# Six context value groups move from the placing stage into the latent routing

## The chip, the cores and the metric

The kernel runs on one core of a Trainium2 chip. The metric is the device time of one launch in microseconds (us). The core has a matmul engine (PE, its weight loads listed as PEld), a vector engine (DVE), an activation engine (ACT), a general-purpose engine that issues the indirect gathers (POOL), and a sequencer for plain transfers (SP). ACT can issue plain transfers too.

## The reference, cut to what matters

The layer ends, for each of 1280 tokens (1024 latent ones, 256 context ones), in a sum over product-key experts:

```
s = einsum('nhpd,pkd->nhpk', q, sub_keys)
s_top, i_top = top_k(s, 16)
...
best, best_pos = top_k(cand, 16)
expert = idx1 * 128 + idx2            # 8 heads x 16 = 128 experts a token
act = gelu(einsum('cd,ced->ce', x_c, u[e_c]))
out = einsum('ce,ced->cd', g_c * act, v[e_c])
```

So a token needs 128 rows of `u` (one dot product each) and 128 rows of `v` (a weighted sum), each of 1024 float32 numbers. A gather of one row for 128 partitions moves 512 KB.

## The kernel before, in words

Tokens are split into ten tiles of 128. Four latent tiles are computed densely, against all experts; four latent and two context tiles (`CONTEXT_GATHER = 2`) gather the rows of the experts they picked. This text is about the second half of that work, the **value sum**, for the two context tiles.

A value group is four tokens. For each of its tokens POOL issues one indirect gather of the 128 rows of `v` that the token picked (one row on each partition), and PE adds them up in eight matmuls (four tokens by two halves of 512 columns), with weights that hold the token's factors in one column. A context tile has 32 groups, so the two have 64. They are computed in two places:

- **In the latent routing** (`routing` with the group LAT, line 1579 on). The class `Values` (line 441) lists the units (tile, group) and cuts the last `LATE_GROUPS` of them off the list (line 452): 64 - 14 = 50 are left. Gathers are in `gather_values` (line 488, the DMA on line 495), products in `value_products` (line 501, matmuls on line 509). The rows lie in a ring of three groups (`VALUE_GROUPS = 3`): the gather of group m waits until the products of group m - 3 are done. POOL has nothing else to do in this stage. PE's products are woven into its other work by hand: 38 of them between the query products (`VALUES_IN_PART`, line 1597), two before each of four transposes of tokens, one after, and **all that are left** at the very end, after the transposes of the expert ids (line 1752). Then ACT takes the sums out of PSUM (`values_out`, line 516, the copy on line 521), SP stores them, and the stage ends with a barrier for all engines. DVE's work in this stage is the top-k search for the latent tokens; its last instruction is the copy of the shares on line 1996.
- **In the placing stage** (`place_weights`, line 2000). This stage turns the routing of the four dense tiles into a dense grid of weights in HBM, in 4 tiles x 8 = 32 steps. In each step DVE makes one-hot rows (lines 2136 to 2151), ACT scales some (2241 to 2255), PE multiplies them (2196), ACT copies the result into the grid (2263). After every eight steps SP stores a tile of the grid, 8 MB (line 2288), the last tile in two halves. Beside that, POOL gathers 24 rows of `u` (line 423) and DVE makes a dot product of each (line 432). The late groups ride along: in every odd step POOL issues four late gathers (line 2092, ring of six rows), and PE makes the products of one group between batches 1 and 2 of the step (`late_products`, line 2171, matmuls on line 2177).

When the last late group is done, at step `LATE_STEPS = 2 * LATE_GROUPS = 28`, ACT asks for the 2 MB load `h2T` into the room in which late rows had landed (2225), copies the sums out of PSUM (2227) and issues four stores of them (2231). Two steps later it waits for these stores and asks for the first two slabs of `u` of the expert stage (2235). Each step's body on ACT runs in the order: scale batch 0, copy batches 2 and 3 of the step before, `late_values` (line 2220), batch 2, copy batches 0 and 1.

The lines that set the sizes and the late part:

```
VALUE_GROUPS = 3                                             # line 437
LATE_GROUPS = 14                                             # line 438
        del self.units[-LATE_GROUPS:]                        # line 452, Values
            values(len(values_left))                         # line 1752, PE, end of routing
        GROUPS = range(P // 4 - LATE_GROUPS, P // 4)         # line 2027, place_weights
        LATE_STEPS = 2 * LATE_GROUPS                         # line 2028
                    if b == 2 and before % 2 and before < LATE_STEPS:
                        late_products(before // 2)
```

Of the kernel before, what the change touches and what calls it, by code (L numbers as in the profile page):

```python
# [434 lines left out]


VALUE_GROUPS = 3
LATE_GROUPS = 14


class Values:
# [4 lines left out]
    def __init__(self, scope, signals, out, last_row):  # L446
# [4 lines left out]
        self.units = [(k, q) for k in range(CONTEXT_GATHER) for q in range(self.GROUPS)]  # L451
        del self.units[-LATE_GROUPS:]
        self.per_tile = [len([u for u in self.units if u[0] == k]) for k in range(CONTEXT_GATHER)]
# [1546 lines left out]
def place_weights(nc, io, keep, scratch, routes, ahead, edge):  # L2000
# [13 lines left out]
    with Scope(nc, "place") as s:  # L2014
# [11 lines left out]
        out = edge.late_row[0]  # L2026
        GROUPS = range(P // 4 - LATE_GROUPS, P // 4)
        LATE_STEPS = 2 * LATE_GROUPS
        ps = [s.psum(f"ps{n}", [P, SLAB]) for n in range(BATCHES)]
# [54 lines left out]
        def _(pool):  # L2084
            def gather_late(rows):
                for i in rows:
                    if i >= 4 * LATE_GROUPS:
                        return
# [73 lines left out]
        def _(pe):  # L2162
# [8 lines left out]
            def late_products(g):  # L2171
# [3 lines left out]
                for t in range(4):  # L2175
                    for half in range(2):
                        last = nc.tensor.matmul(
                            v_ps[QUAD * t:QUAD * (t + 1), half * SLAB:(half + 1) * SLAB], factor_col[:, g % 2, t, :],
                            late_row[(4 * g + t) % LATE_RING][:, half * SLAB:(half + 1) * SLAB],
                            start=(g == 0), stop=(g == LATE_GROUPS - 1), tile_position=(0, QUAD * t))  # L2180
                last.then_inc(values_done, 1)
# [20 lines left out]
        def _(act):  # L2202
            def factor_column(g):
                if g >= 2:
                    act.wait_ge(values_done, g - 1)
                    nc.scalar.activation(factor_col[:, g % 2, :, GROUPS[g - 2]], factorT[:, 0:4], ACT.Copy, scale=0.0)
                q = GROUPS[g]
                nc.scalar.activation(factor_col[:, g % 2, :, q], factorT[:, 4 * q:4 * q + 4], ACT.Copy)\
                  .then_inc(column_ready, 1)
# [10 lines left out]
            def late_values(before):  # L2220
                if before % 2 == 0 and before // 2 + 1 < LATE_GROUPS:
                    factor_column(before // 2 + 1)
                if before == LATE_STEPS:
                    act.wait_ge(values_done, LATE_GROUPS)
                    nc.scalar.dma_start(keep["acc"][:, :, :].rearrange("p t n -> p (t n)").rearrange("p (k n) -> p k n", k=KD),
                                        scratch["h2T"]).then_inc(edge.h2_in, 16)
                    nc.scalar.activation(out, v_ps[:, :], ACT.Copy).then_inc(late_ready, 1)
                    act.wait_ge(late_ready, 1)
                    for t in range(4):
                        rows = slice(QUAD * t + GROUPS[0], QUAD * (t + 1))  # L2230
                        nc.scalar.dma_start(scratch["ffn"][CTX.first + 1][rows, :], out[rows, :]).then_inc(late_stored, 16)
                if before == LATE_STEPS + 2:
                    act.wait_ge(late_stored, 64)
                    for n in range(2):
                        nc.scalar.dma_start(edge.u_raw[:, n, :, :], io["uT"][n]).then_inc(edge.u_in[n], 16)
# [885 lines left out]
```

## Time and profile before

| what | value |
|---|---|
| median of 3 runs | 3383.41 us (3379.23 to 3384.15) |
| the profiled execution's own time | 3384.96 us |
| its span in the profile | 3383.1 us |
| latent routing, value sums of the context | about 1000 to 1386 us of the span |
| placing | 1386 to 1608 us |
| experts | 1609 us to the end |

The profile is of one execution; its time and its span differ by 1.9 us, which lies around the first and the last instruction. All places in time below are microseconds from the start of the span. A line such as `1372.50 0.94 POOL L495 ... [0.30 <-issue]` reads: start, duration, engine, line of the kernel, and in brackets how long the engine had been idle before it and what ended that.

### The profile page before, as it was taken

What the parts mean: (1) busy time and instruction counts of PE and PEld (TensorE: products, weight loads), DVE (VectorE), ACT (ScalarE), POOL (GpSimd) and SP (SyncE); (2) the same over time, 40 slices, a digit from 0 to 9 for tenths busy, and PEclk for the clock granted to TensorE, in tenths of its full rate; (3) what the DMA queues carried; (4) which work ended last, traced back from release to release, by engine and by line L of the source; (5) the groups of instructions that cost most, each with busy time, mean ns of one, the idle gap of its engine ahead of it and who ended that gap; (6) DMA issues with size and microseconds to landing.
All of it is one profiled execution on the core that took longest, in us unless ns stands there. A gap on an engine that the chain in (4) does not pass through costs nothing.

```text
span 3383.1 us, 46093 instructions
## 1 busy us (share of the span) xinstructions
PE 3094.1 (91%) x15031; PEld 2033.5 (60%) x15031; DVE 2658.1 (79%) x5943; ACT 1058.5 (31%) x1909; POOL 1984.7 (59%) x1674
## 2 busy tenths in 40 slices
PE   6989899799899998677699999999999999999996
PEld 4747345666454444455455677776677767677674
DVE  2328899787587999798698878887788888787788
ACT  4741344465121111577211222222222222222222
POOL 0000577444454566543588777787777777777771
PEclk8989999999999999899899999999999999999998
DMA  9441788765967888799999999999999999999997
GB/s 337 174 147 61 250 305 298 208 204 162 356 242 268 298 290 320 289 360 360 355 387 384 411 413 413 413 413 411 413 413 413 413 412 413 413 414 413 410 412 309
DMA packets 365084, 1131.17 MB, mean 334 GB/s; under 512 B 31945, under 2 KB 98761, under 8 KB 356609
## 3 DMA queue, kind: packets, MB, share of 16 engines
q0 software_dynamic: 221184, 805.40, 62.4%
q1 hardware_dynamic: 135248, 316.40, 24.6%
q10 hardware_dynamic: 8496, 7.44, 0.7%
q8 instruction: 80, 1.31, 0.2%
q14 instruction: 76, 0.61, 0.1%
HBM read 1075.93 MB, written 53.19 MB: 334 GB/s over the span
## 4 chain that ended last, share of the span: by engine, by line
PE 25%; DMA 11%; POOL 6%; issue 5%; DVE 4%; ACT 0%; POOLq 0%; SPq 0%; DVEq 0%; ACTq 0%
PE exp_a_ps L2601 12%; DMA exp_value_row<-in_v_rows,exp_v_id 9%; PE exp_o_ps L2628 8%; PE exp_v_ps L2585 4%; POOL exp_value_row L2757 3%; PE exp_o_ps L2633 1%; POOL exp_more_row L2746 1%; POOL exp_value_row L2746 1%; DMA exp_value_row<-in_u_rows,edge_id_and_dot 1%; POOL edge_row L2746 1%; POOL edge_u_raw L2746 1%; DVE keep_acc L2892 1%; DVE exp_value_row L2811 1%; DVE exp_u_lo L2775 1%; DVE edge_u_raw L2811 0%
## 5 line engine op out<-in xcount | busy, mean ns | idle before, releaser
L423 POOL DMA_INDIRECT ahead_row<-in_u_rows,keep_tables x194 | 273.4, 1409 | 555.4 <-POOLq L102 346.9
L2757 POOL DMA_INDIRECT exp_value_row<-in_v_rows,exp_v_id x448 | 492.3, 1099 | 162.0 <-issue 133.0
L2601 PE MATMUL exp_a_ps<-exp_xT_hi,exp_u_hi 128*128 128x512 f32 x1024 | 411.2, 402 | 29.2 <-DVE exp_u_lo L2775 23.6
L2601 PE MATMUL exp_a_ps<-exp_xT_lo,exp_u_hi 128*128 128x512 f32 x1024 | 401.5, 392 | 0.0
L2601 PE MATMUL exp_a_ps<-exp_xT_hi,exp_u_lo 128*128 128x512 f32 x1024 | 400.5, 391 | 0.0
L2746 POOL DMA_INDIRECT edge_row<-in_u_rows,edge_id_and_dot x224 | 304.0, 1357 | 103.7 <-issue 46.0
L2684 ACT ACTIVATE exp_hidden<-exp_a_ps 128x512 f32<-128x512 f32 x128 | 76.6, 598 | 911.2 <-PE exp_a_ps L2601 911.2
L2892 DVE TENSOR_TENSOR keep_acc<-exp_o_ps,keep_acc 128x1024 f32<-128x1024 f32 x250 | 305.6, 1222 | 59.9 <-PE exp_o_ps L2628 51.3
L2628 PE MATMUL exp_o_ps<-exp_v_hi,exp_w_hi 128*128 128x512 f32 x896 | 288.1, 403 | 6.6 <-DVE keep_acc L2941 6.6
L2628 PE MATMUL exp_o_ps<-exp_v_lo,exp_w_hi 128*128 128x512 f32 x896 | 282.9, 397 | 0.0
L2628 PE MATMUL exp_o_ps<-exp_v_hi,exp_w_lo 128*128 128x512 f32 x896 | 280.6, 394 | 0.0
L2601 PEld LDWEIGHTS exp_a_ps<-exp_xT_hi,exp_u_hi 128*128 128x128 f32 x1024 | 193.1, 189 | 116.8 <-issue 48.0
L432 DVE CUSTOM_DVE_ANT_0 ahead_row<-ahead_row,ahead_x 128x1024 f32<-128x1024 f32 x194 | 230.7, 1219 | 23.5 <-DMA ahead_row<-in_u_rows,keep_tables 23.2
L2585 PE MATMUL exp_v_ps<-exp_value_row,exp_hot 128*32 128x512 f32 x1792 | 220.1, 604 | 22.4 <-DMA exp_value_row<-in_v_rows,exp_v_id 22.3
L1572 PE MATMUL queries_q_ps<-mix_featT,queries_slab 128*128 128x512 f32 (+1 forms) x640 | 230.3, 513 | 0.0
L495 POOL DMA_INDIRECT val_row<-in_v_rows,keep_tables x136 | 146.4, 1076 | 127.2 <-PE route_lat_h_ps L509 66.0
L2628 PEld LDWEIGHTS exp_o_ps<-exp_v_hi,exp_w_hi 128*128 128x128 f32 x896 | 164.6, 189 | 89.8 <-issue 47.7
L2601 PEld LDWEIGHTS exp_a_ps<-exp_xT_hi,exp_u_lo 128*128 128x128 f32 x1024 | 193.3, 189 | 41.7
L2601 PEld LDWEIGHTS exp_a_ps<-exp_xT_lo,exp_u_hi 128*128 128x128 f32 x1024 | 193.4, 189 | 39.8 <-issue 1.7
L737 PE MATMUL proj_lat_ps<-mix_featT,heads_early_room 128*128 128x512 f32 x448 | 196.3, 596 | 1.8 <-ACTq L796 1.8
L2654 ACT ACTIVATE exp_u_hi<-exp_u_raw 128x1024 fp32r<-128x1024 f32 x126 | 132.7, 1053 | 199.8 <-DMA exp_u_raw<-in_uT 199.8
L2866 DVE TENSOR_TENSOR exp_hidden<-exp_hidden,exp_g_raw 128x512 f32<-128x512 f32 x112 | 77.7, 694 | 148.3 <-ACT exp_hidden L2684 148.2
(455 smaller groups left out, 6487.5 us busy)
## 6 DMA issues: line engine op xcount, KB each, us to landing
exp_u_raw<-in_uT SPq DMA_DIRECT2D x126, 512.0 KB, 6.7
exp_v_raw<-in_v_rows SPq DMA_DIRECT2D x56, 1024.0 KB
exp_g_raw<-scratch_g SPq DMA_DIRECT2D x64, 512.0 KB, 7.9
scratch_g<-place_grid SPq DMA_DIRECT2D x3, 8192.0 KB, 45.8
proj_ctx_mod_slab<-in_w_mod SPq DMA_DIRECT2D x8, 2048.0 KB, 11.9
heads_early_room<-in_w_in SPq DMA_DIRECT2D x10, 1024.0 KB, 11.2
mod_slab<-in_w_mod SPq DMA_DIRECT2D x4, 2048.0 KB, 20.1
queries_slab<-in_w_q SPq DMA_DIRECT2D x4, 2048.0 KB, 25.4
```

What stands on the lines that cost most here:

```text
L423: nc.gpsimd.indirect_dma_start(out=row, out_offset=None, in_=io["u_rows"], in_offset=bass.IndirectOffsetOnAxis(ap=ahead.keep["expert_id"]. ...
L432: nc.vector.tensor_tensor_reduce(out=row, in0=row, in1=ahead.x[:, n // SLOTS - ahead.first, :], scale=1.0, scalar=0.0, op0=ALU.mult, op1=A ...
L495: nc.gpsimd.indirect_dma_start(out=val.rows[slot][:, t, :], out_offset=None, in_=io["v_rows"].rearrange("a b n -> (a b) n"), in_offset=bas ...
L737: last = nc.tensor.matmul(ps[C * (ct % 2) + c][:, 0:width], early.slab(a, ct // 2)[:, k, ct % 2 * P:(ct % 2 + 1) * P], hT[:, k, g.at + at: ...
L1572: last = nc.tensor.matmul(q_ps[:, 0:width], slab[:, k, ct * P:(ct + 1) * P], h2T[:, k, at:at + width], start=(k == 0), stop=(k == KD - 1))
L2585: mm = nc.tensor.matmul(v_ps[QUAD * t:QUAD * (t + 1), half * SLAB:(half + 1) * SLAB], hot[:, i % 2, t, :], value_row[:, 4 * (i % 2) + t, h ...
L2601: mm = nc.tensor.matmul(a_ps[e][:, :], u[part][:, e, k, :], xT[xp][:, k, :], start=(k == 0 and part == 0 and xp == 0), stop=(k == KD - 1 a ...
L2628: mm = nc.tensor.matmul(o_ps[t % 2][:, c, :], w[1 - parity][part][:, e, t * P:(t + 1) * P], v[1 - parity][xp][:, e, c * SLAB:(c + 1) * SLA ...
L2654: nc.scalar.activation(u[0][:, e, :, :], raw_u(n, e), ACT.Copy).then_inc(u_hi_ready, 1)
L2746: nc.gpsimd.indirect_dma_start(out=row, out_offset=None, in_=io["u_rows"] if mode != "last" else io["v_rows"].rearrange("a b n -> (a b) n" ...
L2757: nc.gpsimd.indirect_dma_start(out=value_row[:, 4 * (j % 2) + t, :], out_offset=None, in_=io["v_rows"].rearrange("a b n -> (a b) n"), in_o ...
L2892: nc.vector.tensor_tensor(acc[:, t, :], o_ps[t % 2][:, :, :].rearrange("p c n -> p (c n)"), acc[:, t, :], ALU.add).then_inc(added, 1)
```

## The change

One constant: fourteen late groups become eight.

```
--- before.py
+++ after.py
@@ -435,7 +435,7 @@
 
 
 VALUE_GROUPS = 3
-LATE_GROUPS = 14
+LATE_GROUPS = 8
 
 
 class Values:
```

With it, `Values` lists 56 groups in place of 50, the placing stage has late groups in its odd steps up to 15 in place of 27, and the load of `h2T`, the store of the late sums (8 rows for each of the four token positions in place of 14) and the two loads of `u` stand at steps 16 and 18 in place of 28 and 30. The number of gathers, products and bytes of the whole kernel stays, except for that split of the stores: the 32 rows of the context's last tile are written whole by the routing's store and then in part by the placing's, as before.

## Rows read from the trace of the kernel before

**Rows 1.** Page, head, part 1 and part 2 (DMA use in 40 slices).
```profile
span 3383.1 us, 46093 instructions
PE 3094.1 (91%) x15031; PEld 2033.5 (60%) x15031; DVE 2658.1 (79%) x5943; ACT 1058.5 (31%) x1909; POOL 1984.7 (59%) x1674
...
GB/s 337 174 147 61 250 305 298 208 204 162 356 242 268 298 290 320 289 360 360 355 387 384 411 413 413 413 413 411 413 413 413 413 412 413 413 414 413 410 412 309
```

**Rows 2.** Windows by stage, routing's end: length, then busy time of each engine.
```profile
core 0: us, PE busy (x) PEld busy (x) DVE busy (x) ACT busy (x) POOL busy (x), PEclk, DMA share, GB/s
...
1340.00:1371.00 31.00, 19.14 (x122) 6.59 (x120) 27.59 (x118) 6.29 (x11) 22.74 (x23) 0.78 1.03 419
1371.00:1386.00 15.00, 5.42 (x32) 1.32 (x32) 0.17 (x2) 1.02 (x1) 1.29 (x3) 0.83 0.51 205
```

**Rows 3.** DVE's timeline: the routing's last instruction and the placing's first.
```profile
1370.35 0.43 DVE L1996 COPY keep_tables<-keep_acc 128x512 f32<-128x512 f32 x1
1385.83 1.77 DVE L2114 COPY place_hot<-keep_acc 128x128 f32<-128x128 f32 x12 [15.05 <-PEq L102]
```

**Rows 4.** PE's timeline, last six groups' products, then ACT's copy and SP's store.
```profile
1351.23 3.67 PE L509 MATMUL route_lat_h_ps<-ahead_row,val_spread 128*32 128x512 f32 x16 [3.30 <-DMA ahead_row<-in_v_rows,keep_tables]
...
1374.30 3.48 PE L509 MATMUL route_lat_h_ps<-val_row,val_spread 128*32 128x512 f32 x16 [4.29 <-DMA val_row<-in_v_rows,keep_tables]
1379.28 1.95 PE L509 MATMUL route_lat_h_ps<-val_row,val_spread 128*32 128x512 f32 x16 [1.50 <-DMA val_row<-in_v_rows,keep_tables]
...
1381.30 1.02 ACT L521 ACTIVATE mix_featT<-route_lat_h_ps 128x1024 f32<-128x1024 f32 x1 [13.37 <-PE route_lat_h_ps L509]
...
1382.35 0.53 SPq L527 DMA_DIRECT2D scratch_ffn<-mix_featT  x1
```

**Rows 5.** POOL's timeline: gathers undisturbed, and the routing's last gather.
```profile
1331.66 0.94 POOL L495 DMA_INDIRECT val_row<-in_v_rows,keep_tables  x1 [0.30 <-issue]
1332.90 0.94 POOL L495 DMA_INDIRECT val_row<-in_v_rows,keep_tables  x1 [0.31 <-issue]
...
1371.43 0.95 POOL L495 DMA_INDIRECT val_row<-in_v_rows,keep_tables  x1 [0.30 <-issue]
```

**Rows 6.** Gathers of line 495 between 1340 and 1386: what POOL and PE waited for.
```profile
  PE route_lat_h_ps L509: 3.5, 3
...
DMA to landing us min/median/max: 6.0/7.8/9.3
```

**Rows 7.** The same line over the whole routing: what POOL waited for.
```profile
  PE route_lat_h_ps L509: 102.9, 37
```

**Rows 8.** Windows of the placing stage, columns as in rows 2.
```profile
1386.00:1443.60 57.60, 45.63 (x341) 37.47 (x342) 56.60 (x135) 44.53 (x126) 35.40 (x30) 0.90 0.75 258
1443.60:1497.50 53.90, 42.67 (x322) 32.60 (x321) 49.06 (x109) 43.03 (x122) 28.16 (x22) 0.94 0.99 371
1497.50:1552.80 55.30, 42.63 (x323) 32.15 (x322) 49.17 (x109) 43.08 (x122) 27.57 (x22) 0.94 0.97 361
1552.80:1580.40 27.60, 20.76 (x157) 15.66 (x157) 24.89 (x55) 21.02 (x59) 9.33 (x7) 0.94 1.04 381
1580.40:1608.00 27.60, 17.31 (x128) 15.97 (x126) 21.08 (x48) 21.39 (x54) 0.00 (x0) 0.94 1.06 356
```

**Rows 9.** DVE's waits from 1497.5 to 1580.4, then two from 1580.4 to 1608.
```profile
DVE place_hot L2141 <- PE place_ps L2196: 8.8, 4, 3.3
...
DVE place_hot L2136 <- PE place_ps L2196: 3.0, 1, 3.0
DVE place_hot L2147 <- PE place_ps L2196: 0.8, 1, 0.8
```

**Rows 10.** PE's waits for late rows from 1497.5 to 1580.4.
```profile
PE place_v_ps L2177 <- DMA keep_acc<-in_v_rows,keep_tables: 7.0, 4, 2.5
PE place_v_ps L2177 <- DMA edge_u_raw<-in_v_rows,keep_tables: 3.0, 1, 3.0
```

**Rows 11.** ACT's timeline at steps 28 and 30: load, copy out, stores, loads.
```profile
1580.39 0.37 ACTq L2225 DMA_DIRECT2D keep_acc<-scratch_h2T  x1
1580.88 1.02 ACT L2227 ACTIVATE edge_u_raw<-place_v_ps 128x1024 f32<-128x1024 f32 x1
1581.93 2.65 ACTq L2231 DMA_DIRECT2D scratch_ffn<-edge_u_raw  x4
...
1595.11 0.39 ACTq L2235 DMA_DIRECT2D edge_u_raw<-in_uT  x1
```

**Rows 12.** Transfers issued between 1553 and 1600: count, size, us to landing.
```profile
scratch_g<-place_grid SPq DMA_DIRECT2D x1, 8192.0 KB, 41.4
scratch_g<-place_grid SPq DMA_DIRECT2D x1, 4096.0 KB, 30.2
keep_acc<-scratch_h2T ACTq DMA_DIRECT2D x1, 2048.0 KB, 11.3
```

## The prediction

> **What bounds the kernel now.** I began with the page. PE is busy for 91% of the span and DVE for 79%, yet the DMA rate stands flat at 413 GB/s through the whole second half [rows 1]. Those are averages over stages with different limits, and the change touches two stages only, so I went on to the busy time by stage, then to the timelines at the seam between the two, and last to the list of waits inside the placing.
>
> At the end of the latent routing the question is which engine arrives last at the barrier. DVE, busy for 27.6 of the last 31 us before 1371 [rows 2], finishes with its copy at 1370.35, and then stands idle for 15.05 us until the placing starts at 1385.83 [rows 3]. What the others wait for is the value stream: each product group on PE is ended by a wait on a gather, the last one starts at 1379.28, ACT copies the sums at 1381.30 and SP stores them at 1382.35 [rows 4]. So the routing's end is set by context values, by 15 us, and not by the routing itself.
>
> Is that stream paced by POOL, by the ring or by the transfers? POOL starts an undisturbed gather every 1.24 us (1331.66 to 1332.90) [rows 5], and the transfers run at 419 GB/s from 1340 to 1371 [rows 2]; both give nearly the same pace. The ring hardly holds POOL up here, 3.5 us in three waits [rows 6], though over the whole routing it held it up for 102.9 us [rows 7]. That earlier slack is not at the change's disposal: the first 47 products have places in PE's order that do not move, and all added ones fall to the call on line 1752, which takes what is left.
>
> In the placing, DVE is the engine that fills the stage: 56.6 of 57.6 us before the first grid store begins. From then on it has holes: 4.8 us, 6.1 us and 2.7 us in the next three stretches [rows 8]. All of the 8.8 us between 1497.5 and 1580.4 are waits for PE [rows 9], and in the same stretch PE itself waited 10.0 us in five places for late rows [rows 10]. The late products cost nothing while no store runs (the first stretch has them too, at one a pair of steps), and something once the grid's 8 MB stores share the DMA engines with them.
>
> **The change, part by part.**
>
> *Added to the routing: 24 gathers and 48 matmuls, six groups.* They all come after the group that now is last, with DVE done and no other work beside them, so their whole time is on the path. Price by POOL: 24 x 1.24 = 29.8 us. Price by bytes: 24 x 0.524 MB = 12.6 MB at 419 GB/s = 30.0 us. Price by what the stream did lately: six products from 1351.23 to 1379.28 are five intervals, 28.05 / 5 = 5.6 us each [rows 4], so 33.7 us, but these intervals had DVE's work and SP's stores of tokens beside them. A ring turn of three groups is 3.7 us of issuing, 7.8 us to landing [rows 6] and 2 to 3.7 us of products [rows 4], 13.5 to 15.2 us, that is 4.5 to 5.1 us a group: just about the issue pace, so it may now and then add a few tenths. I take 31 us, between 29.8 and 33.7 and nearer the two prices that are free of other work. The copy on ACT, the store and the barrier behind it stay, only later. The tail's weights are already there, so nothing else on PE or ACT moves.
>
> The Trainium skill, "DMA: Bandwidth & Descriptors", section Specifications, puts the HBM limit of one core at about 358 GB/s. The trace has 419 GB/s in the very stretch that counts, so I side with the trace; what the rule would make of it is a rival below.
>
> *Taken from the placing: the same six groups in steps 17 to 27.* PE loses the products; they were hidden except where their rows came late. Without them DVE's four waits should go: -8.8 us [rows 9]. The cover for the rest is DVE's own work, 49.17 + 24.89 us in the two stretches [rows 8], which is the floor, so no more than 8.8 us can come back there. The least is 0, if these waits were for a PE or ACT that was late for other reasons; I take 8.5, since PE's 10.0 us of waits [rows 10] match them. POOL's 24 gathers there cost nothing: it was idle for half of the time.
>
> *Moved from step 28 to step 16:* the load of h2T, the copy out and four store issues. On ACT they stand from 1580.39 to 1584.58, 4.2 us [rows 11], and DVE paid 3.0 + 0.8 us for it [rows 9]. The same is paid 12 steps earlier: net 0. Behind the waiting instruction on ACT are batch 2 and two grid copies, for which PE and then DVE wait. From step 30 to step 18: two load issues, and before them the wait for the four stores. The only new neighbour is the second 8 MB grid store, which SP asks for at about the same moment. Now the third store and the half store are open beside it, the 2 MB load takes 11.3 us [rows 12], and ACT gets from 1584.58 to 1595.11 without a visible wait [rows 11]. I take 0, with 0 to 8 us for a longer queue. Nobody is waiting for these loads at the start of the experts; getting them early earns nothing. The grid's last half store and the first key gathers of the experts meet less traffic: 0 to 2 us of gain, of which I take none.
>
> *Everything before and behind is shifted,* not changed: same bytes, same order.
>
> Sum: +31 - 8.5 = +22.5 us. The profiled run took 3384.96 us, 1.5 above the median of the runs shown, so its 3407.5 corresponds to a median of **3406 us**.
>
> **The rivals.**
>
> *A, the placing returns nothing* (the holes stay, since grid stores slow the u rows or since PE's clock and ACT's scaling are what makes PE late). For it: ACT is busy for 43 of 55 us there, not far from DVE [rows 8]. Against: the first stretch has the same work, no store, and 1.0 us of holes. Time: 3383.4 + 31 = 3414.4.
>
> *B, ACT stalls at step 18.* The four small stores queue on ACT's row behind the 2 MB load, with a fresh 8 MB store beside them. If ACT's transfers had to wait until that store was through, 41.4 us from its issue [rows 12] and some 13 us of step time in between, ACT would stand still for up to 28 us; DVE would follow. I price it at 5 to 15 us more: 3411 to 3421. Against it are the 11.3 us of the load beside two other stores. The Trainium skill ("DMA: Bandwidth & Descriptors", section Queues, rings and completion order) says that each engine goes round robin between queue rows, packet by packet; by that rule B would not happen, and the 11.3 us agree with it.
>
> *C, HBM's limit decides the tail.* If the stream can only hold the 355 to 360 GB/s that four slices in the middle of the page show [rows 1], 12.6 MB take 35 us, and the sum is +35 - 8.5: 3410. This is what the rule of the skill's Specifications would give. Against it: 419 GB/s in rows 2.
>
> *D, not slower: PE sets the tail's pace.* If the rows of the added groups had landed when PE comes to them, each would cost only its products, 1.95 us [rows 4], or 11.7 us for six; less 8.5 in the placing that is +3.2 us, 3386.6, within what can be told from no change. It decides if PE runs from product to product with no DMA wait. What speaks for it is POOL's 102.9 us of slack [rows 7]; what speaks against it is that with three slots the slack can't be stored up, and that PE waits before the last two groups already [rows 4].
>
> *E, the change doesn't do what it says.* Both lists come from one constant, so six groups would have to vanish. I give it nothing of its own.
>
> **How the numbers follow.** About 0.2% (7 us) is what a measurement of this kernel can tell from no change. Forecast (tail 30 to 34 us, placing back 6 to 10: 3400 to 3410): 0.66. A: 0.12. B: 0.08. C: 0.07. D: 0.03. Something that pays more back than I see, at the start of the experts or in the DMA-bound rounds: 0.04, 3393 to 3400, of which a quarter is within 0.2% or faster. Range: tail at its least with the full return and 2 us more gives 3383.4 + 29.8 - 10.8 = 3402; I go to 3398 for the last case, and up to 3417 for A with the tail at 33.7. Slower by over 0.2%: everything but D and that quarter, 0.96; same 0.03; faster 0.01.
>
> **What the changed profile would show.** DVE's idle time at the seam, 15.05 us now, at 46 us; six more pairs of gather runs and product groups with 5.0 to 5.6 us between them and DMA at about 415 GB/s; the placing 8 to 9 us shorter (from 222 to about 213.5 us), with no DVE waits behind late rows from step 17 on; ACT's block of 4.2 us at step 16 and the loads of u one pair of steps later. The prediction is wrong if the added groups come at under 4.5 us each, if DVE's holes in the second half of the placing remain, or if ACT waits before line 2235.

## The result and the profile after

The changed kernel takes 3403.9 us in the median of four runs (3398.4 to 3404.83), the kernel before 3381.32 us in four (3375.0 to 3384.15). The ratio is 1.0069, with a 95% interval of 1.0056 to 1.0082: **22.6 us slower**, where 22.5 had been forecast. The profiled execution of the changed kernel is the shortest of its four (3398.4 us, span 3396.1 us), and that of the kernel before (3384.96 us, span 3383.1 us) took longer than any of its four runs, so the two spans differ by 13.0 us only. By stage these are +30.1 us at the seam, -14.9 in the placing, and -2.2 because DVE's search in the routing happened to end earlier; the experts took 1773 us in both. That the difference of two profiles is not the difference of two kernels matters below.

First the seam between routing and placing. DVE's timeline of the changed kernel:

```profile
1368.12 0.43 DVE L1996 COPY keep_tables<-keep_acc 128x512 f32<-128x512 f32 x1
...
1413.66 1.77 DVE L2114 COPY place_hot<-keep_acc 128x128 f32<-128x128 f32 x12 [45.11 <-PEq L102]
```

DVE's search ends where it ended before, within 2.2 us, and then DVE idles for 45.11 us in place of 15.05 [rows 3]. PE's timeline shows what the 30 us are, the products of the six added groups:

```profile
1377.15 1.95 PE L509 MATMUL route_lat_h_ps<-val_row,val_spread 128*32 128x512 f32 x16 [1.64 <-DMA val_row<-in_v_rows,keep_tables]
1382.14 3.49 PE L509 MATMUL route_lat_h_ps<-ahead_row,val_spread 128*32 128x512 f32 x16 [3.05 <-DMA ahead_row<-in_v_rows,keep_tables]
1387.13 1.95 PE L509 MATMUL route_lat_h_ps<-val_row,val_spread 128*32 128x512 f32 x16 [1.51 <-DMA val_row<-in_v_rows,keep_tables]
1392.12 3.61 PE L509 MATMUL route_lat_h_ps<-val_row,val_spread 128*32 128x512 f32 x16 [3.04 <-DMA val_row<-in_v_rows,keep_tables]
...
1407.10 1.95 PE L509 MATMUL route_lat_h_ps<-val_row,val_spread 128*32 128x512 f32 x16 [1.51 <-DMA val_row<-in_v_rows,keep_tables]
```

Read the starts, not the durations: 4.99 us from each to the next, six intervals to the last one, 29.95 us. Each group of products is preceded by a wait for a gather. The windows view of a part of this tail, with length, busy times, PE's granted clock, DMA share and GB/s, shows DVE at nothing and the transfers at the rate of rows 2:

```profile
1371.00:1396.00 25.00, 14.35 (x80) 3.42 (x80) 0.00 (x0) 0.00 (x0) 18.26 (x20) 0.80 1.03 419
```

Then the placing. It runs from 1413.66 to 1622.9, 209.3 us, where it took 224.2. DVE's waits from 1525 to 1621 are all that is left of the 8.8 us and 3.8 us of [rows 9]:

```profile
DVE place_hot L2136 <- PE place_ps L2196: 0.5, 1, 0.5
DVE place_hot L2147 <- PE place_ps L2196: 0.2, 1, 0.2
```

ACT's timeline shows the moved block, at step 16 and 18 now, and the transfers issued from 1505 to 1560 how the load fared beside the fresh grid store:

```profile
1521.58 0.37 ACTq L2225 DMA_DIRECT2D keep_acc<-scratch_h2T  x1
1522.58 1.02 ACT L2227 ACTIVATE edge_u_raw<-place_v_ps 128x1024 f32<-128x1024 f32 x1
1523.63 1.86 ACTq L2231 DMA_DIRECT2D scratch_ffn<-edge_u_raw  x4
...
1534.90 0.39 ACTq L2235 DMA_DIRECT2D edge_u_raw<-in_uT  x1
```

```profile
scratch_g<-place_grid SPq DMA_DIRECT2D x1, 8192.0 KB, 37.6
keep_acc<-scratch_h2T ACTq DMA_DIRECT2D x1, 2048.0 KB, 9.7
```

No wait stands before line 2235, and the 2 MB load lands in 9.7 us beside an 8 MB store, in place of 11.3 [rows 12].

### The profile page after: what moved, and what is told of

Its sections match the earlier page's. It is cut to its first block, busy times and chain, and to the rows that moved or that the text cites. A ratio compares the mean times of both kernels' runs of the same rounds, so it can differ in the third digit from the quotient of the medians.

```text
span 3396.1 us, 46075 instructions
## 1 busy us (share of the span) xinstructions
PE 3093.4 (91%) x15031; PEld 2032.5 (60%) x15031; DVE 2658.1 (78%) x5943; ACT 1056.6 (31%) x1897; POOL 1984.7 (58%) x1674
## 4 chain that ended last, share of the span: by engine, by line
PE 28%; DMA 11%; issue 5%; POOL 5%; DVE 3%; ACT 0%; POOLq 0%; SPq 0%; DVEq 0%; ACTq 0%
PE exp_a_ps L2601 13%; DMA exp_value_row<-in_v_rows,exp_v_id 10%; PE exp_o_ps L2628 9%; PE exp_v_ps L2585 4%; PE exp_o_ps L2633 2%; POOL exp_value_row L2757 1%; POOL exp_value_row L2746 1%; POOL exp_more_row L2746 1%; POOL edge_row L2746 1%; DVE edge_u_raw L2811 1%; POOL edge_u_raw L2746 1%; DMA exp_final_row<-scratch_x 0%; DVE exp_u_lo L2775 0%; DVE keep_acc L2892 0%; ACT exp_hidden L2684 0%
## 5 line engine op out<-in xcount | busy, mean ns | idle before, releaser
L423 POOL DMA_INDIRECT ahead_row<-in_u_rows,keep_tables x194 | 280.5, 1446 | 550.9 <-POOLq L102 344.4
L2746 POOL DMA_INDIRECT edge_row<-in_u_rows,edge_id_and_dot x224 | 291.6, 1302 | 104.4 <-issue 44.3
L495 POOL DMA_INDIRECT val_row<-in_v_rows,keep_tables x152 | 161.8, 1064 | 132.3 <-PE route_lat_h_ps L509 65.4
L2628 PEld LDWEIGHTS exp_o_ps<-exp_v_hi,exp_w_lo 128*128 128x128 f32 x896 | 168.7, 188 | 40.7
```

What stands on the lines that cost most here:

```text
L423: nc.gpsimd.indirect_dma_start(out=row, out_offset=None, in_=io["u_rows"], in_offset=bass.IndirectOffsetOnAxis(ap=ahead.keep["expert_id"]. ...
L495: nc.gpsimd.indirect_dma_start(out=val.rows[slot][:, t, :], out_offset=None, in_=io["v_rows"].rearrange("a b n -> (a b) n"), in_offset=bas ...
L2628: mm = nc.tensor.matmul(o_ps[t % 2][:, c, :], w[1 - parity][part][:, e, t * P:(t + 1) * P], v[1 - parity][xp][:, e, c * SLAB:(c + 1) * SLA ...
L2746: nc.gpsimd.indirect_dma_start(out=row, out_offset=None, in_=io["u_rows"] if mode != "last" else io["v_rows"].rearrange("a b n -> (a b) n" ...
```

## The experiments

The table has fourteen rows: twelve kernels, two of them measured twice. "Placing" is the time from DVE's first instruction of that stage (line 2114) to its first of the expert stage (line 2771), "seam" DVE's idle time just before the placing, each from the one profiled execution of the kernel.

| kernel | groups in routing, late groups | median us, runs | ratio to before (95%) | seam | placing |
|---|---|---|---|---|---|
| before | 50, 14 | 3381.32, 4 | 1 | 15.05 | 224.2 |
| before again | 50, 14 | 3376.36, 12 | 0.9991 (0.998 to 1.0003) | 17.33 | 219.3 |
| changed | 56, 8 | 3403.9, 4 | 1.0069 (1.0056 to 1.0082) | 45.11 | 209.3 |
| changed again | 56, 8 | 3401.16, 6 | 1.0065 (1.0045 to 1.0085) | 47.12 | 209.4 |
| routing alone | 56, 14 | 3412.18, 6 | 1.0095 (1.0078 to 1.0112) | 46.37 | 221.1 |
| placing alone | 50, 8 | 3372.89, 12 | 0.9976 (0.9964 to 0.9988) | 16.59 | 212.6 |
| block at 28 | 56, 8 | 3402.37, 6 | 1.0066 (1.0049 to 1.0084) | 47.61 | 209.7 |
| four late | 60, 4 | 3422.18, 5 | 1.0128 (1.0112 to 1.0144) | 67.54 | 207.4 |
| half rows | 56, 8 | 3398.58, 4 | 1.005 (1.0034 to 1.0065) | 42.74 | 210.9 |
| products without rows | 50, 14 | 3374.82, 12 | 0.9982 (0.9973 to 0.9992) | 16.72 | 216.1 |
| woven 56 | 56, 8 | 3375.81, 12 | 0.9994 (0.9983 to 1.0005) | 2.22 | 210.6 |
| woven 56, later | 56, 8 | 3385.58, 12 | 1.0019 (1.0011 to 1.0028) | 13.29 | 212.8 |
| woven 50 | 50, 14 | 3378.71, 12 | 0.9999 (0.9989 to 1.0009) | 3.05 | 220.4 |
| woven by two | 50, 14 | 3373.78, 12 | 0.9985 (0.9973 to 0.9997) | 4.30 | 218.5 |

The kernel before had a median of 3379.3 to 3379.7 us in the 17 to 29 runs beside the experiments; their ratios are to these. "Before again", the same kernel as its reference, came out at 0.9991, so a difference of 3 us needs no cause.

### The two halves of the change, each alone

Routing alone, on the kernel before:

```
 LATE_GROUPS = 14
+ROUTING_LEAVES = 8
-        del self.units[-LATE_GROUPS:]
+        del self.units[-ROUTING_LEAVES:]
```

> Half of the change: the routing sums 56 groups, the placing still sums all fourteen of its own (six groups are summed twice, the placing's store overwrites the routing's, so the output is whole). Theory (six groups in the bare tail at 5.0 us each): 30 us slower than before, seam idle of DVE 45 us as in the changed kernel, placing unchanged at about 223 us. Rival (the changed kernel's other part is worth more than I gave it, and the tail too): 33 us or more.

Placing alone is the same edit on the changed kernel, with `ROUTING_LEAVES = 14`.

> The other half: the placing sums only eight groups, the routing still only 50, so the value sums of 24 context tokens are left out. Theory as predicted (only DVE's waits for late rows go): 8.5 us faster. Rival 1 (rival A of the prediction, nothing comes back): 0 us. Rival 2 (the profiled pair, placing shorter by 14.9 us, is what holds): 13 to 15 us faster. The sum of this run and the routing-alone run should give the changed kernel's +22.6 within 3 us.

Routing alone cost 1.0095, or 32 us (26 to 38), with the seam at 46.37 us and the placing at 221.1: the theory. Placing alone gave 0.9976, or 8 us (4 to 12), with the seam unchanged: the predicted value, and neither nothing nor 15. The two together are +24 us; the changed kernel on the same chip has +22. The parts add up within what can be measured. The profile of "routing alone" repeats the seam of the changed kernel with the placing as it was: that the tail costs 30 us by itself is shown, not only argued.

### The moved block put back

```
-                if before == LATE_STEPS:
+                if before == 28:
...
-                if before == LATE_STEPS + 2:
+                if before == 30:
```

> The changed kernel with the load of h2T, the store of the late sums and the loads of u put back to steps 28 and 30. Theory as predicted (the block costs the same 4 us wherever it stands): equal to the changed kernel within 1 us. Rival (the block is cheaper at step 16, which would explain why the profiled placing got shorter by more than DVE's waits for late rows): 3 to 5 us slower than the changed kernel, that is +26 to +28 against before.

3402.37 against 3401.16 us for the changed kernel, placing 209.7 against 209.4. The two intervals are each 6 to 7 us to either side, so the times alone could not tell 3 to 5 us from nothing; the placings in the profiles can. The block's place is worth nothing that they show, which settles the stall of rival B too: ACT did not wait before line 2235, and a kernel in which the block could not have met the fresh grid store is no faster.

### The two kernels again

> The changed kernel once more, on the chip of the three others, as their reference. Theory: +22.5 us against before in the median, and a placing stage between 208 and 214 us in the profile. If the placing's length varies by several us between executions of one kernel, the profiled difference of 14.9 us is in part chance.

> The kernel before once more, for a second profile of it. Theory (the profiled placing of 224 us was a long draw, as that execution was 4 to 5 us over the median of its kernel): placing near 220 us, ratio 1. Rival (224 us is typical): placing at 224 us again, and then the placing's gain from the change is 14 to 15 us and the tail's price 36.

The changed kernel repeats: 1.0065, placing 209.4. The second profile of the kernel before has a placing of 219.3 us: its first profile, 224.2, was a long draw. One can see in PE's timeline what differs. In the first profile the late products of step 9 begin so, two matmuls a row:

```profile
1452.27 0.85 PE L2177 MATMUL place_v_ps<-edge_u_raw,keep_tables 128*32 128x512 f32 x2 [1.99 <-DMA keep_acc<-in_v_rows,keep_tables]
...
1452.83 1.14 PE L2177 MATMUL place_v_ps<-edge_u_raw,keep_tables 128*32 128x512 f32 x2
1452.94 1.09 PE L2177 MATMUL place_v_ps<-keep_acc,keep_tables 128*32 128x512 f32 x2
```

and in the second profile, after an even longer wait:

```profile
1453.69 0.63 PE L2177 MATMUL place_v_ps<-edge_u_raw,keep_tables 128*32 128x512 f32 x2 [2.41 <-DMA keep_acc<-in_v_rows,keep_tables]
1453.72 0.63 PE L2177 MATMUL place_v_ps<-keep_acc,keep_tables 128*32 128x512 f32 x2
```

The same two matmuls take 1.1 us or 0.63: PE's lower clock level (1.2 GHz) against its upper one (2.4 GHz), after the same kind of wait. In the first profile the granted clock is 1.00 during the wait and 0.50 from 1452.6 to 1455.7, while the products run; in the second it stays at 1.00. A group's 16 matmuls come out at 1.95 us, or at 2.5 to 3.6 when slowed. In the first profile five of the fourteen groups ran slow, in the second two. The stretch from the first grid store on has a granted clock of 0.94 in the first [rows 8], 0.97 in the second and 1.00 in the changed kernel's (and again in its repetition). The second profile of before, then the changed kernel:

```profile
1444.40:1498.20 53.80, 41.59 (x327) 32.89 (x326) 49.64 (x109) 43.45 (x123) 27.11 (x23) 0.97 1.00 373
```

```profile
1471.50:1521.00 49.50, 38.56 (x317) 31.02 (x316) 48.01 (x105) 41.77 (x116) 24.89 (x20) 1.00 1.02 381
```

The change is not the whole cause of that: "placing alone" and "woven 56, later", with eight late groups, had two slowed groups each in this stretch and placings of 212.6 and 212.8 us. What a late row costs can be read from DVE's next wait for PE, again in step 9, first profile, then second:

```profile
1456.99 1.22 DVE L2141 TENSOR_TENSOR place_hot<-keep_iota,place_cols 128x1024 f32<-128x1024 f32 x1 [2.36 <-PE place_ps L2196]
...
1456.76 1.23 DVE L2141 TENSOR_TENSOR place_hot<-keep_iota,place_cols 128x1024 f32<-128x1024 f32 x1 [1.14 <-PE place_ps L2196]
```

PE waited 1.99 us for the row and DVE then 2.36 us with the slowed products; PE waited 2.41 us and DVE only 1.14 us with the fast ones. The other late rows after the first grid store agree, in all profiles of these kernels: where the clock stayed up, DVE waited 1.3 us less than PE had (1.9 us gave 0.6, 2.8 gave 1.5), and where it fell, 0.1 to 0.4 us more (3.02 gave 3.34). So DVE's own work covers more than half of a wait of 2 us, and the lower clock uses that cover up. Of the 14.5 us that DVE waited at line 2141 in the first profile, 13.4 stand behind the five slowed groups.

The number of slowed groups orders the placings too. With eight late groups: none, 209.3 to 209.7 us; one, 210.6 and 210.9; two, 212.6 and 212.8. With fourteen: two, 218.5 and 219.3; three, 220.4 and 221.1; five, 224.2. From the first to the last that is 1.6 us a slowed group with eight, 1.8 with fourteen. Why a group is slowed in one execution and not in the next is open.

### What in the placing costs the time: rows or products

```
-                    if i >= 4 * LATE_GROUPS:
+                    if i >= 4 * 8:
...
-                for i in range(4 * g, 4 * g + 4):
+                for i in range(4 * g, 4 * g + 4) if g < 8 else ():
                     pe.wait_ge(edge.late_in[i % LATE_RING], 16 * (i // LATE_RING) + 16)
```

> The kernel before, whose placing makes all fourteen groups' products but gathers the rows of only the first eight and waits for no others (six groups sum stale rows, so 24 tokens of the output are other numbers). Theory (the placing's gain is the late rows: PE's waits for them and what the waits do to PE's granted clock; the products themselves are hidden): placing 210 to 212 us, as with eight groups, kernel 8 to 11 us faster than before. Rival (the products on PE are the cost): placing stays at 219 to 224 us.

0.9982, or 6 us faster (3 to 9). Placing 216.1, which lies between the two theories and needs a look inside: its steps before 16, where nothing was edited, had two slowed groups in this execution (3.45 and 3.55 us). DVE's waits from 1495 to 1590, with all six groups' products still on PE, are these:

```profile
DVE place_hot L2136 <- PE place_ps L2196: 2.4, 1, 2.4
DVE place_hot L2147 <- PE place_ps L2196: 1.0, 1, 1.0
DVE place_hot L2141 <- PE place_ps L2196: 0.5, 2, 0.2
```

The 0.5 us is what is left behind the products in the edited steps, where the five profiles with fourteen late groups and their rows have 1.5 to 8.8 us. In these steps the products are hidden and the rows were the cost, as the prediction had it. But the first two lines, 3.4 us at 1581, are the moved block at step 28: it costs what it did before, where the profiles with eight late groups have 0.4 to 2.1 us for it. So the return of the change is not all in the rows, and the speedup is smaller than the theory's 8 to 11 us; the interval touches only its lower end. What makes the block cheaper in the changed kernel is not shown.

### More groups in the tail

```
-LATE_GROUPS = 8
+LATE_GROUPS = 4
```

> Four late groups in place of eight, so ten groups more than before in the routing's tail, and the placing's late steps end before the first grid store. Theory: another 4 x 5.0 = 20 us in the seam (to 65 us), placing 4 us shorter than in the changed kernel (DVE's 4.8 us of holes from 1443.6 to 1497.5 us go as well): +38 us against before. Rival (the holes there are not from late rows): placing unchanged, +42 us.

The seam grew by 20.4 us over that of the changed kernel's second profile (67.54 - 47.12), 5.1 a group. The placing got 2 us shorter, half of what I expected: with PE's clock up, groups four to seven cost little (0.6 and 1.5 us of DVE's waits in the two profiles of the changed kernel). Together +43 us, with an interval of 38 to 49 that leaves both the theory's 38 and the rival's 42 standing; it is the profiles that show part of the theory's 4 us.

### What paces the tail

```
+        wide = D if m < val.GROUPS + 15 else D // 2
...
-            out=val.rows[slot][:, t, :], out_offset=None, in_=io["v_rows"].rearrange("a b n -> (a b) n"),
+            out=val.rows[slot][:, t, 0:wide], out_offset=None, in_=io["v_rows"].rearrange("a b (h n) -> (a b h) n", n=wide),
```

> The changed kernel, but the last nine groups in the routing fetch 2 KB in place of 4 KB for each partition (from other rows, the right half of the sums is left stale), so their transfers carry half the bytes. Theory 1 (POOL's issue of 1.245 us a gather paces the tail, the bytes only fit under it): gathers and products stay 5.0 us a group apart, the seam shrinks only by the shorter landing of the last one, 2 to 4 us. Theory 2 (the transfers pace it at 420 GB/s and hold POOL back through the ring): the products come closer than 5.0 us, the seam shrinks by more than 5 us. Kernel against before: +18 to +20 by theory 1, under +15 by theory 2.

The windows view from 1371 to 1396 has half the rate, and PE's timeline the same pace:

```profile
1371.00:1396.00 25.00, 12.69 (x87) 3.33 (x80) 0.00 (x0) 0.00 (x0) 18.91 (x21) 0.86 0.73 209
```

```profile
1389.41 3.25 PE L510 MATMUL route_lat_h_ps<-val_row,val_spread 128*32 128x512 f32 x16 [2.97 <-DMA val_row<-in_v_rows,keep_tables]
1394.54 1.95 PE L510 MATMUL route_lat_h_ps<-ahead_row,val_spread 128*32 128x512 f32 x16 [1.88 <-DMA ahead_row<-in_v_rows,keep_tables]
1399.55 3.15 PE L510 MATMUL route_lat_h_ps<-val_row,val_spread 128*32 128x512 f32 x16 [3.06 <-DMA val_row<-in_v_rows,keep_tables]
```

With 209 in place of 419 GB/s and landings of 3.7 us in place of 6.2, the groups are still 5.0 us apart, and the seam is 2.4 us shorter than in the first profile of the changed kernel (3.9 shorter than the mean of the four with 56 groups): theory 1. The time, +17 us (11 to 22), reaches into both theories and decides nothing. POOL's issue alone holds the tail at four gathers of 1.245 us a group: POOL never waited for the ring here. The full rows fit under it with nothing to spare: their DMA share is 1.03 against 0.73, and three short ring waits of 0.45 to 0.71 us stand between POOL's gathers.

### Weaving the groups in earlier

The added groups are dear because they fall behind the last score. POOL has 103 us of ring waits before that. Two versions move products in front of the last scores, one on the changed kernel with its 56 groups (the first of the two added lists), one on the kernel before with 50 (the second):

```
-    TURN_VALUES = (3, 0)
-    VALUES_IN_PART = {(0, 2): 4, (1, 0): 5, (1, 1): 5, (2, 0): 6, (2, 1): 6, (3, 0): 6, (3, 1): 3, (3, 2): 3}
+    TURN_VALUES = (2, 1)
+    VALUES_IN_PART = {(0, 2): 5, (1, 0): 6, (1, 1): 6, (2, 0): 7, (2, 1): 8, (3, 0): 7, (3, 1): 4, (3, 2): 4}
+    VALUES_IN_PART = {(0, 2): 5, (1, 0): 6, (1, 1): 6, (2, 0): 7, (2, 1): 8, (3, 0): 6, (3, 1): 3, (3, 2): 3}
```

> The changed kernel with its 56 groups woven earlier into PE's query products: 32 groups of the first context tile by slab 2 in place of slab 3, 15 of the second in slab 3 in place of 6, so that nine are left behind the query products in place of eighteen. Theory (the six groups cost 30 us only since they fall into the bare tail; POOL's 103 us of ring waits earlier can carry them): DVE's seam idle returns from 45 us to about 15, and the kernel is 8 to 12 us faster than before, since the placing's gain is all that remains. Rival (PE is full until 1320 us, so nine more products of 1.94 us there delay the scores and DVE with them): DVE's last instruction 15 to 20 us later, kernel within 5 us of before or slower.

> The kernel before (fourteen late groups) with the same kind of weaving: 44 groups in the query products, six left behind them in place of twelve. Theory: the value stream ends before DVE does, the seam idle falls from 15 us to a few us, kernel 10 to 13 us faster than before, placing unchanged near 222 us. Rival (PE full until 1320 us): DVE ends later by up to 12 us and the gain is 0 to 3 us.

Both times the seam closed, to 2.22 and 3.05 us, and both times the rival was right about the kernel: 0.9994 and 0.9999. DVE's timeline of "woven 56" shows where it went:

```profile
1386.15 0.43 DVE L1996 COPY keep_tables<-keep_acc 128x512 f32<-128x512 f32 x1
1388.79 1.77 DVE L2114 COPY place_hot<-keep_acc 128x128 f32<-128x128 f32 x12 [2.22 <-PEq L102]
```

DVE's search now ends at 1386.6, 17 us later than the mean of the ten profiles without weaving (1366.5 to 1371.1); its list of waits has 39.8 us for scores where it had 24.8, and 5.3 where it had 2.5 for ACT's exponentials (line 1794), behind which ACT's copies of the tokens stand. In the kernel before PE is busy for 219 of the 220 us from 1100 to 1320, where its last scores are made, so products put in front of them delay them: nine more by 15 to 18 us (the last ones start at 1333.6, in the two profiles of the changed kernel at 1315.8 and 1318.7). "Woven 50", with six more, starts them at 1330.6 in place of 1318.2 and 1318.7 and ends its search at 1380.8, for the same reason. The changed kernel's loss is repaired in full this way, and no more.

I then tried to find the balance. "Woven by two", on the kernel before:

```
-    VALUES_IN_PART = {(0, 2): 4, (1, 0): 5, (1, 1): 5, (2, 0): 6, (2, 1): 6, (3, 0): 6, (3, 1): 3, (3, 2): 3}
+    VALUES_IN_PART = {(0, 2): 4, (1, 0): 5, (1, 1): 5, (2, 0): 6, (2, 1): 6, (3, 0): 6, (3, 1): 4, (3, 2): 4}
```

> The kernel before with only two products more in the last slab (4 and 4 in place of 3 and 3 in its second and third part), so ten groups behind the query products in place of twelve. From the other weavings: a product costs DVE's end 1.94 us, since PE is full until it has made the last scores, and takes 5.0 us off the stream's end. Theory: DVE's last instruction 4 us later, value stream 6 us earlier, seam idle from 16 to about 6 us, kernel 5 to 7 us faster than before. Rival (the weaving gives back what it gains at any dose): within 2 us of before.

"Woven 56, later", on the changed kernel, again with the turn moved:

```
+    TURN_VALUES = (2, 1)
+    VALUES_IN_PART = {(0, 2): 4, (1, 0): 6, (1, 1): 6, (2, 0): 8, (2, 1): 8, (3, 0): 6, (3, 1): 3, (3, 2): 4}
```

> The changed kernel with 45 groups woven into the query products in place of 47, and fewer of them early on, so eleven are left behind. Theory (by 1.94 us a product before PE's last scores and 5.0 us a group after them, ten to eleven left are the balance): seam idle about 8 us, placing 210 us, kernel 5 to 8 us faster than before and 2 us faster than the first weaving of 56. Rival: within 2 us of the first weaving or of before.

"Woven by two" has the seam at 4.30 us and its search ending at 1377.2; the ratio is 0.9985 (0.9973 to 0.9997), 5 us faster than before (1 to 9). It is the only version with the whole output whose interval lies below 1. That does not clear it of the rival's "within 2 us", with "before again" at 0.9991. Its working was off on both sides: the two products moved the end of DVE's search by about 8 us in place of 4 (it waited 6.3 us for ACT's exponentials, against 0.3 to 2.5), and the placing began 4 us earlier in place of 6.

"Woven 56, later" failed: 1.0019, slower than "woven 56" by 8 to 10 us. Its search ends at 1385.1, and its stream ends later, with two groups more behind. In products moved, nine, six, seven and two, the search ended 17, 11, 16 and 8 us later than the mean without weaving: at 1.95 us a product this fits the first two only. The three kernels with the turn moved share a longer wait for scores, 39.8, 37.9 and 37.7 us in seven places, where "woven by two" has 25.0 in five as before. The number of products in front of the last score is not all that counts; how much of it is the turn and how much the middle parts is not shown.

## Why the prediction was right

*What bounds the routing's end.* Right. The value stream set it, and all six groups were added to it: seams of 45.11, 47.12, 47.61 and 46.37 us in four profiles with 56 groups, mean 46.6, against 15.05, 17.33, 16.59 and 16.72 in four with 50, mean 16.4. The difference is 30.1 us; "31, between 29.8 and 33.7" had been forecast. Of the two prices that came out alike, the half rows showed that POOL's holds with the other one taken away. Rival C (a limit in the rate of HBM, 35 us) is out: 419 GB/s again. The Trainium skill, "DMA: Bandwidth & Descriptors", Specifications, has the limit of one core at about 358 GB/s. The trace does not agree. Rival D (products at their own 1.95 us) is out: 4.99 us apart, each behind a wait.

*What the placing gives back.* Right in kind and near in sum, but its parts are not those of the prediction. The step said that "DVE's four waits should go: -8.8 us" and "no more than 8.8 us can come back there". They did go. Seven profiles with eight late groups have placings of 209.3 to 212.8 us, mean 210.8; five with fourteen (and their rows) have 218.5 to 224.2, mean 220.7. That is 9.9 us, and 11.7 between "routing alone" and the mean of the changed kernel's two profiles. DVE is busy for 201 us of the placing in all of them, so these 9.9 us are DVE's idle time, and the timelines of the twelve profiles sort it by place:

| DVE's idle time in the placing, means | fourteen late groups | eight late groups | difference |
|---|---|---|---|
| steps 17 to 27, waits behind late rows | 4.2 (1.5 to 8.8) | 0 | 4.2 |
| waits at the moved block | 3.4 | 1.1 | 2.3 |
| before the first instruction of the experts | 5.6 | 4.7 | 0.9 |
| steps up to 15, the same code in both | 6.3 | 3.9 | 2.4 |

The 8.8 us were the largest of five draws, three slowed groups in one execution. The mechanism that the prediction named is worth about half of that. The rest came from the block, for which it took "net 0", and, with 2.4 us, from steps that the change doesn't touch and that had more slowed groups in the profiles with fourteen late groups; no run shows whether that is chance. Rival A, nothing back, is refuted by "placing alone".

*The moved block.* Right in that its place doesn't matter, by the version that puts it back, and rival B did not happen. But it got 2.3 us cheaper in the mean, as the table shows.

*The sum.* 30.1 - 9.9 = 20.2 us from the profiles, 22.6 and 21.5 from the times; the 1.3 to 2.4 us between them are inside the intervals, which are 4 to 7 us to either side. The match to a tenth is luck: the tail was 1 us cheaper than taken and the placing gave 1 to 3 us more than taken, both in the same direction, while the times came out at the forecast. That 8.5 us were close to what the placing gave is in part luck as well: too much for the late rows, nothing for the rest.

## What to carry to other kernels

Work that is "off the path" in one stage may be bare in the next: before moving it, look which engine arrives last at the barrier, and whether the place that the order of instructions gives to the added part has any cover. Here the last arrival already was the kind of work that was added, so its full price showed, four gathers at POOL's 1.245 us a group. And filling an engine's idle time by way of a busy one is not free: POOL had 103 us of ring waits to give, but each group woven in earlier put 1.95 us of products on PE ahead of the scores that DVE was waiting for. Last, a wait read from one profile is one draw: the 8.8 us that the prediction took were 1.5 to 5.1 in the four other profiles with fourteen late groups.

## What the runs showed of the hardware

The same 16 matmuls behind a wait of about 2 us ran in 1.95 us or in 2.5 to 3.6 us, at the upper or the lower clock level, in different executions of one and the same kernel (granted clock 0.97 and 0.94 over the stretch). In step 9 of the first profile the granted clock was 1.00 through the wait of 1.99 us and 0.50 right behind it. Two to five slowed groups go with placings of 218.5 to 224.2 us. The first pair of profiles, five slowed groups against none, has a placing shorter by 14.9 us in place of the mean 9.9: that is about 5 of the 9.6 us by which its spans (13.0 us apart) fell short of the times (22.6), and the routing's earlier end is another 2.2.

The rate of the gathers was 419 GB/s over 25 us with no other data transfers beside them, at a pace of 4.99 us for four. With rows of 2 KB in place of 4 KB the rate halved to 209 and the pace stayed: a gather of 128 rows keeps POOL busy for 0.94 or 0.95 us and comes 1.25 us after the last one at either size.
